# Operand and weight rows of a two-block transformer kernel moved to other SBUF addresses, and its last residual loaded in twelve pieces

## The chip, the cores and the metric

The kernel runs on one NeuronCore of a Trainium2 chip. The metric is the device time of one execution in microseconds (us). PE is the matrix engine (TensorE), DVE the vector engine, ACT the scalar engine, POOL is GpSimd and SP the engine whose queue issues all DMAs here. A partition is one of the 128 lanes of SBUF, the on-chip memory; addresses below are bytes within a partition.

## What is computed

Two transformer blocks over 256 tokens of width 2048 (the first sees 16 more learned tokens ahead of them), all in float32:

```python
# block 1
h = concat([meta, x])                                  # 272 tokens
m = hybrid_mixer(rmsnorm(h, g_pre_mix), w_in, ...)     # two kinds of attention and a convolution; w_out at the end
h = h + rmsnorm(m, g_post_mix)
g = causal_dwconv(rmsnorm(h) @ w_gate, w_conv)         # convolution over three tokens
f = (silu(g) * (rmsnorm(h) @ w_up)) @ w_down           # 2048 -> 5632 -> 2048
h = (h + rmsnorm(f, g_post_ffn))[:, 16:]               # 256 tokens
# block 2
p = rmsnorm(h) @ w_in_2                                # latent attention, top-k attention, gates
h = h + (sigmoid(g1) * (a @ w_branch_a) + sigmoid(g2) * (b @ w_branch_b)) @ w_out_2
q = rmsnorm(h) @ peer_w_q                              # product keys: 16384 experts, top 16 for each of 8 heads
h = h + sum over chosen experts of coef * v_emb        # done densely: U (16384 x 2048), then V
out = rmsnorm(h) * g_final
```

## The kernel before

It is written directly, engine by engine, with semaphores. Nearly all of its time is a stream of weights: the list `PLAN` cuts every weight matrix into chunks of 128 partitions x 1024 columns (8 weight blocks of 128x128, also called rows k here), 1116 in all. Each chunk goes through the same steps, in the order of `PLAN`:

1. SP loads it into `raw` (4 buffers, `RN`), when DVE is done with the chunk four before it (`load`, L725).
2. ACT rounds it to the matmul type float32r into `wh` (3 buffers, `SN`; `cut`, L2091), when PE is done with the chunk three before it.
3. DVE takes the remainder, `wl = raw - wh` (`cut`, L1332).
4. PE multiplies. The operand is split the same way into a high and a low half (`xh`, `xl`), so every 128x128 block takes three matmuls (function `three`):

```python
t.matmul(o, lh, rh, ...)     # L772: weights wh, moving operand xh
t.matmul(o, lh, rl, ...)     # L773: weights wh, moving operand xl
t.matmul(o, ll, rh, ...)     # L774: weights wl, moving operand xh
```

Each has a weight load of its own, which runs while the matmul before it does. ACT and DVE do all else (norms, softmax, convolutions) between their chunks, at slots that tables lay down ahead of time. The order of the work on each engine is fixed when the program is built.

The stages, in this order, with the operand that moves, its columns, and the span of time in the profiled execution:

- first input projection (`in1`), `x`, 272 columns, to 347 us; attention and convolution are mixed into it;
- output projection (`out1`), `y`, 258 columns, 350 to 446 us;
- gate and up (`guk`: the first seven tiles side by side, one k after another; `gu`: the others, tile by tile), `x`, 258 columns for gate tiles and 256 for up tiles, 453 to 958 us;
- down (`down`), `a`, 256 columns, 964 to 1203 us;
- second input projection (`in2k`: seven tiles side by side; `in2`), `x`, 256 columns, 1211 to 1640 us, with the second attention mixed into it; then the branches and the second output projection, to 1815 us;
- `wq` and U, `x`, 256 columns, from 1815 us; from 2410 us U and V alternate; from 2734 us V alone, in which the weights `wh`, `wl` are the moving operand of 512 columns and the coefficients `ch`, `cl` (128x128) are what is loaded.

A gate tile needs `TQ` = 258 columns rather than 256 because the convolution looks two tokens back (`Q0` = 14).

Where buffers start, in the built program (bytes in a partition): `wh` 23200, `wl` 35488, `xh` 47776, `xl` 65440, `yh` 113248, `yl` 129760, `ah` 113248 + 176, `al` 158560 + 176. A chunk is 4096 bytes, so modulo 256 every weight row of 512 bytes starts at 160. `xh` has rows of 276 words (1104 bytes) from its start for the first block, rows of 1024 bytes from word 48 for the second input projection, and from word 28 for `wq` and U (function `normed_at`). `y` has rows of 258 words. "Difference" below is the start of the operand's row less the start of the row of its own weights, modulo 256.

The state of the residual after the second attention is written to HBM (`spill`) and comes back into the `G` tensor as `fin`, with the last gain as `gain`, by two DMAs that SP issues in the middle of the last V half (L757, L758).

Of the kernel before, what the change touches and what calls it, by code (L numbers as in the profile page):

```python
# [17 lines left out]
KT = 16  # L18
# [3 lines left out]
Q0 = 14  # L22
TQ = T1 - Q0
FT = 44
# [44 lines left out]

RN, SN = 4, 3  # L70
CH = 1024

# [100 lines left out]
V1 = AT["V", 0, 1]  # L173
UEND = [AT["U", j, 1] - U0 for j in range(128)]
# [265 lines left out]
def build(nc, A, out):  # L440
# [31 lines left out]
    yh = alloc(mixed_scope, "yh", [128, 16, TQ], F32R)  # L472
    yl = alloc(mixed_scope, "yl", [128, 16, TQ], F32R)
# [24 lines left out]
    ah, al = [alloc(ffn, f"a{i}", [128, 64 + FT * S], F32R)[:, 44:44 + FT * S].rearrange("p (k t) -> p k t", t=S) for i in "hl"]  # L498
# [16 lines left out]
    cosr = alloc(at, "cosr", [128, 2, S])  # L515
    sinr = alloc(at, "sinr", [128, 2, S])
# [32 lines left out]
    oh = alloc(hot_scope, "oh", [128, 8, 2, 128])  # L549
    hot_scope.close()  # L550
    ch, cl = [alloc(px, f"c{i}", [128, 64 + 2 * S], F32R)[:, 28:28 + 2 * S].rearrange("p (n t) -> p n t", t=S) for i in "hl"]
# [30 lines left out]
    hots = [(oh[:, i, 0, :], oh[:, i, 1, :]) for i in range(8)]  # L582
# [137 lines left out]
    def _(y):  # L720
# [19 lines left out]
        for i in range(RN, NCH):  # L740
# [29 lines left out]
    def _(t):  # L770
# [9 lines left out]
        def chunk(i, o, k0, n, rhs, start, stop, ready=None):  # L780

            taken(i)
            for k in range(k0, k0 + n):
                if ready:
                    ready(k)
                c = slice(128 * (k - k0), 128 * (k - k0) + 128)
                last = three(o, wh[:, i % SN, c], wl[:, i % SN, c], *rhs(k), start and k == k0, stop and k == k0 + n - 1)
            last.then_inc(gemm, 1)
# [5 lines left out]
        def pair(i0, outs, rhs, norm):  # L794

            for part in PAIR:
                for i, k in part:
# [5 lines left out]
                    c = slice(128 * (k % 8), 128 * (k % 8) + 128)  # L803
# [1844 lines left out]
```

## Time and profile before

| | |
|---|---|
| median of 3 runs | 3346.98 us (3345.13 to 3348.75) |
| the profiled execution, its own time | 3345.66 us |
| its span, first to last instruction | 3343.8 us |
| PE busy | 3309.1 us, 24828 matmuls |
| DVE busy | 2173.6 us |
| ACT busy | 1678.6 us |
| mean granted clock of PE | 0.995 |
| HBM read | 585.00 MB |

Matmuls overlap in the records: one lasts 0.28 us, but the next starts 0.11 us after it. How fast PE goes is read from how far apart matmuls start, not from their duration, and "busy" says only that some matmul was under way.

### The profile page before, as it was taken

What the parts mean: (1) busy time and instruction counts of PE and PEld (TensorE: products, weight loads), DVE (VectorE), ACT (ScalarE), POOL (GpSimd) and SP (SyncE); (2) the same over time, 40 slices, a digit from 0 to 9 for tenths busy, and PEclk for the clock granted to TensorE, in tenths of its full rate; (3) what the DMA queues carried; (4) which work ended last, traced back from release to release, by engine and by line L of the source; (5) the groups of instructions that cost most, each with busy time, mean ns of one, the idle gap of its engine ahead of it and who ended that gap; (6) DMA issues with size and microseconds to landing.
All of it is one profiled execution on the core that took longest, in us unless ns stands there. A gap on an engine that the chain in (4) does not pass through costs nothing.

```text
span 3343.8 us, 60220 instructions
## 1 busy us (share of the span) xinstructions
PE 3309.1 (99%) x24828; PEld 3136.3 (94%) x24828; DVE 2173.6 (65%) x3664; ACT 1678.6 (50%) x2630; POOL 99.1 (3%) x131
## 2 busy tenths in 40 slices
PE   8999999999999999999999999999999999999998
PEld 8999999999999999899999999999999998888887
DVE  8875367666665477565576698878755555555655
ACT  5454455444444454545455444566644445544544
POOL 0000100000000000000000000122100000000000
PEclk9999999999999999999999999999999999999999
DMA  6433445555566655445566556544555555556554
GB/s 210 139 121 120 158 160 184 184 185 184 180 187 195 195 171 175 136 137 164 183 192 202 196 193 195 178 150 148 162 193 193 192 193 193 193 194 227 189 189 158
DMA packets 164000, 593.12 MB, mean 177 GB/s; under 512 B 18448, under 2 KB 19088, under 8 KB 163344
## 3 DMA queue, kind: packets, MB, share of 16 engines
q1 hardware_dynamic: 163728, 589.27, 54.1%
q8 instruction: 198, 3.24, 0.4%
q14 instruction: 74, 0.61, 0.1%
HBM read 585.00 MB, written 4.19 MB: 176 GB/s over the span
## 4 chain that ended last, share of the span: by engine, by line
PE 98%; DMA 1%; DVE 1%; ACT 0%; SPq 0%; issue 0%; ACTq 0%
PE ps L772 31%; PE ps L773 31%; PE ps L774 30%; PE ps L1260 2%; PE ps L840 1%; PE ps L1061 0%; DMA raw<-in_peer_v 0%; PE ps L1033 0%; PE ps L882 0%; DMA ht<-in_hT 0%; PE ps L810 0%; PE ps L1088 0%; PE ps L842 0%; PE ps L1087 0%; PE ps L1098 0%; PE ps L1083 0%
## 5 line engine op out<-in xcount | busy, mean ns | idle before, releaser
L2091 ACT CAST wh<-raw 128x1024 fp32r<-128x1024 f32 (+2 forms) x1116 | 1163.1, 1043 | 1268.7 <-PE ps L774 1264.6
L1332 DVE TENSOR_TENSOR wl<-raw,wh 128x1024 fp32r<-128x1024 f32 (+2 forms) x1116 | 1347.6, 1209 | 509.4 <-ACT wh L2091 506.9
L772 PE MATMUL ps<-xh,wh 128*128 128x256 f32 (+2 forms) x5184 | 1473.9, 284 | 19.9 <-DVE xl L1341 10.2
L773 PE MATMUL ps<-xl,wh 128*128 128x256 f32 (+2 forms) x5184 | 1454.8, 281 | 0.0
L774 PE MATMUL ps<-xh,wl 128*128 128x256 f32 (+2 forms) x5184 | 1454.3, 281 | 0.0
L772 PEld LDWEIGHTS ps<-xh,wh 128*128 128x128 f32 x5184 | 983.1, 190 | 26.0 <-issue 10.7
L773 PEld LDWEIGHTS ps<-xl,wh 128*128 128x128 f32 x5184 | 983.6, 190 | 2.2
L774 PEld LDWEIGHTS ps<-xh,wl 128*128 128x128 f32 x5184 | 981.1, 189 | 0.0
L772 PE MATMUL ps<-wh,ch 128*128 128x512 f32 x1024 | 400.6, 391 | 1.4 <-DVE cl L2028 1.4
L773 PE MATMUL ps<-wl,ch 128*128 128x512 f32 x1024 | 401.7, 392 | 0.0
L774 PE MATMUL ps<-wh,cl 128*128 128x512 f32 x1024 | 400.8, 391 | 0.0
L2028 DVE TENSOR_TENSOR cl<-G,ch 128x256 fp32r<-128x256 f32 x256 | 109.0, 426 | 245.4 <-ACT ch L2463 245.4
L772 PEld LDWEIGHTS ps<-wh,ch 128*128 128x128 f32 x1024 | 193.8, 189 | 43.4 <-DVE wl L1332 1.8
L774 PEld LDWEIGHTS ps<-wh,cl 128*128 128x128 f32 x1024 | 191.9, 187 | 42.5
L773 PEld LDWEIGHTS ps<-wl,ch 128*128 128x128 f32 x1024 | 192.3, 188 | 39.2
L772 PE MATMUL ps<-ah,wh 128*128 128x256 f32 x704 | 193.6, 275 | 0.0
L773 PE MATMUL ps<-al,wh 128*128 128x256 f32 x704 | 193.6, 275 | 0.0
L774 PE MATMUL ps<-ah,wl 128*128 128x256 f32 x704 | 193.6, 275 | 0.0
L2463 ACT CAST ch<-G 128x256 fp32r<-128x256 f32 x256 | 103.2, 403 | 167.6 <-PE ps L774 167.6
L773 PEld LDWEIGHTS ps<-al,wh 128*128 128x128 f32 x704 | 132.1, 188 | 0.0
L774 PEld LDWEIGHTS ps<-ah,wl 128*128 128x128 f32 x704 | 132.1, 188 | 0.0
L772 PEld LDWEIGHTS ps<-ah,wh 128*128 128x128 f32 x704 | 132.1, 188 | 0.0
(361 smaller groups left out, 3169.6 us busy)
## 6 DMA issues: line engine op xcount, KB each, us to landing
raw<-in_peer_u SPq DMA_DIRECT2D x256, 512.0 KB, 4.3
raw<-in_peer_v SPq DMA_DIRECT2D x256, 512.0 KB, 4.4
raw<-in_w_in SPq DMA_DIRECT2D x186, 512.0 KB, 3.7
raw<-in_w_up SPq DMA_DIRECT2D x82, 512.0 KB, 4.2
raw<-in_w_gate SPq DMA_DIRECT2D x80, 512.0 KB, 4.1
raw<-in_w_down SPq DMA_DIRECT2D x80, 512.0 KB, 4.0
raw<-in_w_out SPq DMA_DIRECT2D x64, 512.0 KB, 3.8
raw<-in_w_branch_a SPq DMA_DIRECT2D x16, 512.0 KB, 3.5
```

The costliest lines, as they stand in the source:

```text
L772: t.matmul(o, lh, rh, start=start, stop=False)
L773: t.matmul(o, lh, rl, start=False, stop=False)
L774: return t.matmul(o, ll, rh, start=False, stop=stop)
L840: t.matmul(dst, qT[rows, c:c + nq], kT[rows, 0:nk], start=True, stop=False)
L1260: t.matmul(ps[5 + n % 3][:, 128 * i:128 * i + 128], b, a, start=True, stop=True).then_inc(hot_mm, 1)
L1332: v.tensor_tensor(wl[:, i % SN, 0:cols(i)], raw[:, i % RN, 0:cols(i)], wh[:, i % SN, 0:cols(i)].bitcast(F32), ALU.subtract).then_inc(lo, 1)
L2028: v.tensor_tensor(cl[:, n % 2, :], G[:, n % 128, :], ch[:, n % 2, :].bitcast(F32), ALU.subtract).then_inc(c_l, 1)
L2091: s.copy(wh[:, i % SN, 0:cols(i)], raw[:, i % RN, 0:cols(i)]).then_inc(hi, 1)
L2463: s.copy(ch[:, n % 2, :], G[:, j, :]).then_inc(c_h, 1)
```

## The change

1. **Wide stages.** For `in1`, `out1` and `gu` each of the 8 weight rows of a chunk starts 144 words (576 bytes) after the one before; the `wh` and `wl` buffers grow from 1024 to 1152 words, and ACT and DVE write them with gaps. The operand of these stages has rows of 272 words (1088 bytes) and starts 28 words (`x`) or 44 words (`y`) into its buffer. The halo grows from 2 to 4 columns (`Q0` = 12), so output projection and gate tiles have 260 columns; up tiles start 4 words into their row, and so do their weights. In `guk` the weights of k start 16 words x (k mod 4) later.
2. **Second input operand.** `x` for the second input projection starts at word 28, not 48. `ah` and `al` become one tensor.
3. **Last residual.** The two DMAs of 128x4096 and 128x2048 words become eight and four of 128x512, one every second chunk, beginning earlier.
4. To pay for the space, cos and sin tables share `gate`, and the one-hot buffers of the expert stage use gaps of `wh`, `wl` and `x` (13 pairs rather than 11).

```diff
-Q0 = 14
+Q0 = 12
+HALO = TQ - S
+PAD_X, PAD_Y, PAD_A, PAD_C = 28, 44, 44, 28
+WIDE = ("in1", "out1", "gu")
+WROW = 144
+PIECE = {AT["V", 10 + 2 * n, 1]: n for n in range(12)}
...
-    wh = alloc(top, "wh", [128, SN, CH], F32R)
-    wl = alloc(top, "wl", [128, SN, CH], F32R)
-    xbuf = [alloc(top, f"x{i}", [128, KT, T1 + 4], F32R) for i in "hl"]
+    wh = alloc(top, "wh", [128, SN, 8 * WROW], F32R)
+    wl = alloc(top, "wl", [128, SN, 8 * WROW], F32R)
+    xbuf = [alloc(top, f"x{i}", [128, KT * (T1 + 4)], F32R) for i in "hl"]
...
-    yh = alloc(mixed_scope, "yh", [128, 16, TQ], F32R)
-    yl = alloc(mixed_scope, "yl", [128, 16, TQ], F32R)
+    yh, yl = [alloc(mixed_scope, f"y{i}", [128, 64 + 16 * T1], F32R)[:, PAD_Y:PAD_Y + 16 * T1].rearrange(
+        "p (k t) -> p k t", t=T1)[:, :, 0:TQ] for i in "hl"]
...
     def normed_at(half, norm):
-        if norm < 2:
-            return xbuf[half][:]
-        o = (48, 28)[norm - 2]
-        return xbuf[half][:].rearrange("p k t -> p (k t)")[:, o:o + KT * S].rearrange("p (k t) -> p k t", t=S)
+        t = T1 if norm < 2 else S
+        return xbuf[half][:, PAD_X:PAD_X + KT * t].rearrange("p (k t) -> p k t", t=t)
+
+    def row_at(w, i, r):
+        name, m, _ = PLAN[i]
+        o = WROW * r + (HALO if name == "gu" and m % 2 else 0) if name in WIDE else 128 * r
+        return w[:, i % SN, o:o + 128]
+
+    def part_at(w, i):
+        name, m, _ = PLAN[i]
+        if name in WIDE:
+            o = HALO if name == "gu" and m % 2 else 0
+            return w[:, i % SN, :].rearrange("p (r c) -> p r c", c=WROW)[:, :, o:o + 128]
+        o = key_row(i)
+        return w[:, i % SN, o:o + cols(i)]
+
+    def key_row(i):
+        name, k, _ = PLAN[i]
+        return 16 * (k % 4) if name == "guk" else 0
...
-            if i == AT["V", 28, 1] + 7:
-                y.wait_ge(d_spill, 16)
-                y.wait_ge(c_l, 128 + 30)
-                y.dma_start(fin, spill).then_inc(d_re, 16)
-                y.dma_start(gain, A["g_final"]).then_inc(d_gf, 16)
+            if i in PIECE:
+                n = PIECE[i]
+                if n == 0:
+                    y.wait_ge(d_spill, 16)
+                y.wait_ge(c_l, 128 + 2 * n + 2)
+                c = slice(512 * (n % 4), 512 * (n % 4) + 512)
+                if n < 8:
+                    y.dma_start(fin[:, n // 4, c], spill[:, n // 4, c]).then_inc(d_re, 16)
+                else:
+                    y.dma_start(gain[:, c], A["g_final"][:, c]).then_inc(d_gf, 16)
...
-        xg = [halves(1, TQ), halves(1, S, 2)]
+        xg = [halves(1, TQ), halves(1, S, HALO)]
...
-            v.tensor_tensor(wl[:, i % SN, 0:cols(i)], raw[:, i % RN, 0:cols(i)], wh[:, i % SN, 0:cols(i)].bitcast(F32),
-                            ALU.subtract).then_inc(lo, 1)
+            v.tensor_tensor(part_at(wl, i), raw_at(i), part_at(wh, i).bitcast(F32), ALU.subtract).then_inc(lo, 1)
...
-            s.copy(wh[:, i % SN, 0:cols(i)], raw[:, i % RN, 0:cols(i)]).then_inc(hi, 1)
+            s.copy(part_at(wh, i), raw_at(i)).then_inc(hi, 1)
```

In the changed program the buffers start at `wh` 23200, `wl` 37024, `xh` 50848 + 112, `xl` 68512 + 112, `yh` 116320 + 176, `yl` 133984 + 176, `a` 116320 + 176. Modulo 256 the first weight row is at 160 and each of these operands at 16, so every difference is 112; only the branches and the second output projection keep 192, and V its own.

The order of the instructions stays as it was on PE, DVE and ACT. It moves on SP, where the last V half is loaded (`raw` is the chunk buffer, `G` holds `fin` and `gain`). SP's queue before, from the last chunk that alternates with U on:

```order
L725 DMA raw<-in_peer_u 128x1024 [waits s_lo] x2
L725 DMA raw<-in_peer_v 128x1024 [waits s_lo] x124
L757 DMA G<-spill 128x4096 [waits s_c_l,s_d_spill]
L758 DMA G<-in_g_final 128x2048
L725 DMA raw<-in_peer_v 128x1024 [waits s_lo] x93
L762 DMA out<-G 128x1024 [waits s_f_out]
```

And the same place of SP's queue in the change; between the fourth row from above and the last but two, the pair of rows goes on in the same way to twelve pieces:

```order
L759 DMA raw<-in_peer_v 128x1024 [waits s_lo] x99
L795 DMA G<-spill 128x512 [waits s_c_l,s_d_spill]
L759 DMA raw<-in_peer_v 128x1024 [waits s_lo] x2
L795 DMA G<-spill 128x512 [waits s_c_l]
...
L797 DMA G<-in_g_final 128x512 [waits s_c_l]
L759 DMA raw<-in_peer_v 128x1024 [waits s_lo] x96
L801 DMA out<-G 128x1024 [waits s_f_out]
```

The 128x4096 and 128x2048 loads stood together behind 124 V chunks; the first small piece now stands behind 99, and two chunks lie between any two pieces.

## Rows read from the trace of the kernel before

**Rows 1.** The page, part 4: the chain that ended last, by engine and line.

```profile
PE 98%; DMA 1%; DVE 1%; ACT 0%; SPq 0%; issue 0%; ACTq 0%
PE ps L772 31%; PE ps L773 31%; PE ps L774 30%; PE ps L1260 2%; PE ps L840 1%; PE ps L1061 0%; DMA raw<-in_peer_v 0%; PE ps L1033 0%; PE ps L882 0%; DMA ht<-in_hT 0%; PE ps L810 0%; PE ps L1088 0%; PE ps L842 0%; PE ps L1087 0%; PE ps L1098 0%; PE ps L1083 0%
```

**Rows 2.** Groups of PE by form: count, busy us, mean ns, idle before.

```profile
L772 PE MATMUL ps<-xh,wh 128*128 128x272 f32 x688 | 205.8, 299 | 9.8 <-DVE wl L1332 9.5 <-DVE xl L1341 0.2
L772 PE MATMUL ps<-xh,wh 128*128 128x258 f32 x704 | 200.0, 284 | 5.0 <-DVE xl L1341 5.0
L772 PE MATMUL ps<-yh,wh 128*128 128x258 f32 x256 | 72.7, 284 | 0.0
```

**Rows 3.** Windows, PE alone: stretch, us, busy (count), clock, DMA share, GB/s.

```profile
34.00:94.00 60.00, 60.00 (x481) 1.00 0.53 174
405.00:440.00 35.00, 35.00 (x294) 1.00 0.55 182
520.00:920.00 400.00, 400.00 (x3330) 1.00 0.56 184
980.00:1180.00 200.00, 200.00 (x1768) 1.00 0.65 193
1880.00:2000.00 120.00, 120.00 (x1061) 1.00 0.57 187
```

**Rows 4.** The same windows view, second input projection.

```profile
1225.00:1245.00 20.00, 20.00 (x172) 1.00 0.57 174
1606.00:1636.00 30.00, 30.00 (x267) 1.00 0.60 186
```

**Rows 5.** Groups of L773 in 1225:1245, 1211:1640 and 1830:2400 us.

```profile
L773 PE MATMUL ps<-xl,wh 128*128 128x256 f32 x57 | 16.0, 281 | 0.0
L773 PE MATMUL ps<-xl,wh 128*128 128x256 f32 x911 | 254.3, 279 | 0.0
L773 PE MATMUL ps<-xl,wh 128*128 128x256 f32 x1471 | 405.4, 276 | 0.0
```

**Rows 6.** Timeline of PE from 1844 us, wq stage: start, us, what.

```profile
1844.33 0.60 PE L1226 MATMUL ps<-ident,ht 128*128 128x128 f32 x4
...
1845.12 0.28 PE L772 MATMUL ps<-xh,wh 128*128 128x256 f32 x1
...
1846.43 0.28 PE L774 MATMUL ps<-xh,wl 128*128 128x256 f32 x1
1846.54 0.28 PE L772 MATMUL ps<-xh,wh 128*128 128x256 f32 x1
```

**Rows 7.** Windows, PE alone, V by itself.

```profile
2760.00:3040.00 280.00, 280.00 (x1237) 1.00 0.59 194
3060.00:3070.00 10.00, 10.00 (x46) 1.00 0.99 406
...
3090.00:3320.00 230.00, 230.00 (x988) 1.00 0.58 188
```

**Rows 8.** The chain in order of time, around 3060 us: start, us, what.

```profile
3057.50 12.21 DMA raw<-in_peer_v
...
3072.53 0.47 PE ps L772
```

**Rows 9.** Timeline of ACT and of PE at the same place.

```profile
3069.74 1.05 ACT L2091 CAST wh<-raw 128x1024 fp32r<-128x1024 f32 x1 [3.59 <-DMA raw<-in_peer_v]
...
3070.75 0.39 PE L774 MATMUL ps<-wh,cl 128*128 128x512 f32 x1
```

**Rows 10.** DMA issues: name, count, KB each, us to landing.

```profile
G<-spill SPq DMA_DIRECT2D x1, 2048.0 KB, 10.7
...
G<-in_g_final SPq DMA_DIRECT2D x1, 1024.0 KB, 12.8
```

**Rows 11.** Windows, all engines (PE, PEld, DVE, ACT, POOL), 60 to 100 us.

```profile
60.00:100.00 40.00, 40.00 (x322) 40.00 (x321) 39.68 (x77) 18.57 (x21) 0.00 (x0) 1.00 0.52 170
```

**Rows 12.** Groups of DVE by form, whole span.

```profile
L1332 DVE TENSOR_TENSOR wl<-raw,wh 128x1024 fp32r<-128x1024 f32 x1062 | 1296.2, 1222 | 475.1 <-ACT wh L2091 472.8
```

More of the change, by code:

```diff
@@ L497, in build @@
     ffn = ExitStack()
-    ah, al = [alloc(ffn, f"a{i}", [128, 64 + FT * S], F32R)[:, 44:44 + FT * S].rearrange("p (k t) -> p k t", t=S) for i in "hl"]
+    ahl = alloc(ffn, "a", [128, PAD_A + 2 * FT * S], F32R)
+    ah, al = [ahl[:, PAD_A + i * FT * S:PAD_A + (i + 1) * FT * S].rearrange("p (k t) -> p k t", t=S) for i in range(2)]
     g_t = alloc(ffn, "g_t", [128, 2, TQ])
@@ L514, in build @@
     perm = alloc(at, "perm", [128, 7, 128])
-    cosr = alloc(at, "cosr", [128, 2, S])
-    sinr = alloc(at, "sinr", [128, 2, S])
+    cosr, sinr = gate[:, 0:2, :], gate[:, 2:4, :]
     rcol = alloc(at, "rcol", [128, 4])
@@ L581, in build @@
     gsum = carve(8)
-    hots = [(oh[:, i, 0, :], oh[:, i, 1, :]) for i in range(8)]
+    spare = [w[:, i, CH:CH + 128] for w in (wh, wl) for i in range(SN)]
+    spare += [x[:, PAD_X + KT * S + 128 * i:PAD_X + KT * S + 128 * i + 128] for x in xbuf for i in range(2)]
+    hots = [(a, oh[:, i, :]) for i, a in enumerate(spare)]
     hots += [(par[:, 256 * i:256 * i + 128], par[:, 256 * i + 128:256 * i + 256]) for i in range(NPAR // 256)]
@@ L785, in chunk @@
                     ready(k)
-                c = slice(128 * (k - k0), 128 * (k - k0) + 128)
-                last = three(o, wh[:, i % SN, c], wl[:, i % SN, c], *rhs(k), start and k == k0, stop and k == k0 + n - 1)
+                last = three(o, row_at(wh, i, k - k0), row_at(wl, i, k - k0), *rhs(k), start and k == k0, stop and k == k0 + n - 1)
             last.then_inc(gemm, 1)
@@ L802, in pair @@
                         t.wait_ge(xlo, 16 * norm + k + 1)
[L803 to L804 removed]
+                    last = three(outs[i], row_at(wh, n, k % 8), row_at(wl, n, k % 8), *rhs[i](k), k == 0, k == 15)
                     if k % 8 == 7:
@@ L1259, in hot_mm_3 @@
                 t.wait_ge(two, tk + 1)
-                t.matmul(ps[5 + n % 3][:, 128 * i:128 * i + 128], b, a, start=True, stop=True).then_inc(hot_mm, 1)
+                t.matmul(ps[5 + n % 3][:, 128 * i:128 * i + 128], b, a.bitcast(F32), start=True, stop=True).then_inc(hot_mm, 1)
         def side_3(name, a):
@@ L1611, in side_g @@
                 v.wait_ge(gu_t, f + 1)
-                v.scalar_tensor_tensor(c1, g1[:, 1:1 + S], w[1], c1, ALU.mult, ALU.add).then_inc(own.up(), 1)
+                v.scalar_tensor_tensor(c1, g1[:, HALO - 1:HALO - 1 + S], w[1], c1, ALU.mult, ALU.add).then_inc(own.up(), 1)
                 v.wait_ge(own.sem, own.n)
-                v.scalar_tensor_tensor(c1, g1[:, 2:2 + S], w[2], c1, ALU.mult, ALU.add).then_inc(gu_c, 1)
+                v.scalar_tensor_tensor(c1, g1[:, HALO:HALO + S], w[2], c1, ALU.mult, ALU.add).then_inc(gu_c, 1)
             elif name == "u":
@@ L2265, in side_g @@
                     s.wait_ge(gu_m, f - 1)
-                s.activation(c1, g_t[:, f % 2, 0:S], ACT.Copy, scale=pc("w_ffn_conv", 3 * f)).then_inc(gu_t, 1)
+                s.activation(c1, g_t[:, f % 2, HALO - 2:HALO - 2 + S], ACT.Copy, scale=pc("w_ffn_conv", 3 * f)).then_inc(gu_t, 1)
             elif name == "conv":
```

16 lines of the change are left out of this document (9 added, 7 removed).

## The prediction

> **What bounds the kernel now.** I read the page's chain first: 98% of the span is PE, and nearly all of that is the three lines of `three` [rows 1]. DVE and ACT are about two thirds and half busy, so a microsecond is gained only if the matmuls follow each other faster or an idle hole in PE closes. Holes are few: PE is busy in every stretch of the windows that I read [rows 3, 4]. So the question is how far apart matmuls start. The windows view gives that: length of the stretch over its count, after taking off the 2.4 matmuls (1.7 for 512 columns) that began before the stretch, because one lasts 0.28 us (0.39) and is counted where it overlaps.
>
> - Down projection (256 columns): 200 us / 1765.6 = 113.3 ns. The U stage gives the same (120/1058.6 = 113.4) [rows 3].
> - First projection (272 columns): 60/478.6 = 125.4 ns. Output projection (258): 35/291.6 = 120.0. Gate and up tiles (258 and 256 alternately): 400/3327.6 = 120.2 [rows 3].
> - V halves (512 columns): 280/1235.3 = 226.7 ns early, 230/986.3 = 233.2 late [rows 7]. 226.7 is twice 113.3, so the fast pace is proportional to columns, 0.443 ns each. By it 272 columns would take 120.4, 260 take 115.1, 258 take 114.2.
>
> The three wide stages thus lose 5 to 7 ns per matmul against a pace that other stages hold, at full granted clock in all of them. What is different there? From the sizes of the buffers in their order of allocation I worked out where the moving operand's row starts relative to the weights' row, modulo 256 bytes. Down projection: 112. Second input projection: 192. wq and U: 112. All have operand rows of 1024 bytes beside weight rows of 512, so the difference is the same for every k. In the wide stages operand rows are 1104 (x) or 1032 (y) bytes, and the difference wanders by 80 or 8 per k.
>
> The pace isn't a matter of the difference alone. The second input projection has a constant 192 and does both: 20/169.6 = 117.9 ns in its first part and 30/264.6 = 113.4 at its end [rows 4]. The duration of one shows it too: 281 ns at the slower pace; over the whole stage the xl matmuls average 279.1 (254.3 us / 911), where wq and U, side work included, have 275.6 (405.4/1471) [rows 5]. At 112 an interruption costs only a short run: after four identity matmuls the starts are 119 ns apart for 11 steps (1845.12 to 1846.43), and the next comes after 0.11 us [rows 6], as all do from there. I read this as two streams, moving operand and next weights, that lock into a free relation if the addresses repeat, and that from 112 always find it.
>
> Against it stands the Trainium skill ("TensorE: Matmul & The Clock Gate", Step-by-step: what each phase is for): the weight load has its own read port and doesn't steal bandwidth from the running matmul. By that, addresses could not matter. The rows differ: the same instruction with the same shape takes 113.3 or 117.9 ns. What it would make of the time is the first rival below.
>
> **The change, part by part.**
> 1. *Wide stages.* Rows of 1088 bytes beside rows of 576: both step by 64 modulo 256, so a matmul and its own weights differ by 112 for every k, and so for y, and for up tiles, where operand and weights both start 16 bytes later. If they lock: first projection 2064 matmuls (three times 688 [rows 2]) x (125.4 - 120.4) = 10.3 us; output projection 768 x (120.0 - 115.1) = 3.8; gate 2112 x (120.2 - 115.1) = 10.8; up 2112 x (120.2 - 113.3) = 14.6. Sum 39.5 us. The two extra columns are already in it: 2880 matmuls x 2 x 0.443 = 2.6 us.
>    Off it: each interruption costs some 14 matmuls x 5 ns = 0.07 us [rows 6]; the attention in the first projection makes about 50 (estimate: five groups for each of ten heads), 3.3 us; changes between gate and up tiles, 2 us (I take half of what 81 changes at 0.05 would cost). DVE has 39.68 of 40 us busy between 60 and 100 us [rows 11]: when a chunk falls from 3.01 to 2.89 us, DVE can't follow there, 1 us. That leaves 33 us.
> 2. *Strided conversions.* wh and wl are written as 8 rows of 128 with gaps. No row shows such a write. A 128x1024 subtraction takes 1222 ns contiguous [rows 12]. Lower bound nothing; upper bound a tenth more for the 86 in the first projection, 86 x 0.122 = 10.5 us, because only there DVE has no cover. In gate and up a chunk has 24 x 115 = 2760 ns, which covers both engines. I take nothing, as the data per lane are the same number of contiguous words in each row.
> 3. *Second input operand* from 192 to 112. 2736 matmuls (three times 912, of which [rows 5] has 911); the stage's mean duration would fall from 279.1 to 275.6, and between 275.6 and 281 lie 4.5 ns of spacing: 2.9 ns x 2736 = 8 us at most, nothing at least (if 112 re-locks no better in a stage that is interrupted every 24 to 48 matmuls). I take 3.5.
> 4. *Twelve pieces.* The 2048 KB and 1024 KB loads stand ahead of a raw load, which then lands after 12.21 us; ACT waits 3.59 us for it and PE's next matmul after 3070.75 starts at 3072.53, 1.78 us where 0.23 is normal: 1.55 us [rows 8 to 10]. And the pace changes at just that place: 226.7 before it, 233.2 after [rows 7]. The rest, 3072.5 to 3332 us, is 1113 matmuls x 6.5 = 7.2 us. A piece is 256 KB per two chunks of 512 KB: 194 GB/s becomes about 243, and the crowded stretch shows 406 GB/s [rows 7], so no stall should follow. One-hot buffers, the shared cos/sin and the joined a tensor add nothing: no engine on the chain waits for them. Sum 8.8 us.
>
> The profiled execution has 3345.66 us (span 3343.8), 1.3 under the median. 3345.7 - 33 - 3.5 - 8.8 = 3300.4; with half of the 1.3, **3301 us**.
>
> **The rivals.**
> - *No address effect.* The paces come from the operand's length or the stage. Then the extra columns cost 2.6 us, the pieces give 1.55 or 8.8: 3337 to 3345 us. For it: no row shows 258 or 272 columns with a constant difference, so none shows them fast over a stretch. Against it: the second input projection and V at two paces. Chance 0.10. The Trainium skill's rule (same page and section as above) would end here.
> - *Only 256-column tiles lock.* 272 and 260 columns don't fit the rhythm that 256 and 512 share; up tiles gain (14.6 less 2), gate, input and output projections only pay 2.6: 3345.7 - 12.6 + 2.6 - 3.5 - 8.8 = 3323. Against it nothing but that no row tests it. Chance 0.13.
> - *One in three is off.* The third matmul of each k runs while the next k's weights load, 576 bytes on: its difference is 48, where at 1024/512 it stays 112. At the slow pace for a third: 39.5 x 2/3 - 4 = 22 us instead of 33: 3311. Chance 0.15.
> - *DVE becomes the bound in the first projection* (part 2's upper bound): 3301 to 3311, inside the others; 0.05.
> - *Slower: V locks badly from its start.* At 2734 us V stands alone at 226.7; nothing in the rows says why it fell there. Had it entered at 233.2, the stretch to 3071 would cost 1487 x 6.5 = 9.7 us, and the 7.2 would not come back. Wide stages locked: 3345.7 - 33 - 3.5 - 1.55 + 9.7 = 3317 (0.07). Wide stages not locked: 3345.7 + 2.6 - 1.55 + 9.7 = 3356 (0.04). It decides the sign when the wide stages bring under 10.7 us.
>
> **How the numbers follow.** The sum as worked out, 3290 to 3306, has 0.46; 3311 has 0.20 with the DVE case; 3317 and 3323 have 0.20; 3337 to 3345 has 0.10; 3356 has 0.04. The range 3290 to 3328 holds 0.84. The low end is the full 39.5 + 8 + 8.8 = 56.3 (3290). 0.2% is 6.7 us, about what a measurement of this kernel can tell. Faster (under 3340): 0.92 and a little less for what I don't see, 0.91; same 0.05; slower 0.04.
>
> **What would show it.** Right: windows give about 120.4 to 121.5 ns in the first projection, 115 in the output projection, 114 to 115 in gate/up, 113.3 to 115 in the second input projection, 226.7 through V to the end, and no long landing near 3000 us. "One in three" shows as 122 and 117; "only 256" as 125, 121 and about 118 in gate/up; no effect as 125, 121, 121. A DVE bound shows as PE idle behind wl. V at 233 from 2700 us on would make 3301 wrong by 17 us.

## The result and the profile after

The changed kernel takes 3343.99 us (median of 12 runs, 3335.44 to 3347.21) where the kernel before takes 3349.9 on the same chip (12 runs, 3341.5 to 3356.02). The medians lie 5.9 us apart; the ratio of the two sets of runs is 0.9977, 95% interval 0.9966 to 0.9988: faster by 4 to 11 us. I had forecast 49 us (3301 against the 3350 measured here, 46 against the 3347 that I started from), and 0.91 for a time under 3340. The direction is right, the size is not, and the time lies outside the range of 3290 to 3328.

The page of the changed kernel, part 4, the chain that ended last (`three` is now L811 to L813):

```profile
PE ps L811 31%; PE ps L812 30%; PE ps L813 30%; PE ps L1297 2%; PE ps L877 1%; PE ps L1098 0%; DVE wl L1369 0%; PE ps L1070 0%; PE ps L919 0%; PE ps L847 0%; PE ps L1125 0%; PE ps L879 0%; PE ps L1124 0%; PE ps L881 0%; PE ps L1135 0%; PE ps L1120 0%
```

The raw load of `peer_v` that stood in the chain of before [rows 1] is gone from it. The rest is the same stream of matmuls. Windows, PE alone (stretch, us, busy and count, granted clock, DMA share, GB/s), over the stretches that [rows 3], [rows 4] and [rows 7] show of before:

```profile
34.00:94.00 60.00, 60.00 (x481) 1.00 0.52 173
405.00:440.00 35.00, 35.00 (x293) 1.00 0.55 183
520.00:920.00 400.00, 400.00 (x3349) 1.00 0.56 185
1225.00:1245.00 20.00, 20.00 (x179) 1.00 0.61 187
2760.00:3040.00 280.00, 280.00 (x1237) 1.00 0.60 202
3060.00:3070.00 10.00, 10.00 (x46) 1.00 0.60 197
3090.00:3320.00 230.00, 230.00 (x1016) 1.00 0.59 191
```

Read as in the prediction (length over the count less 2.4, less 1.7 in V):

| stage | before, ns per matmul | forecast | after |
|---|---|---|---|
| first projection | 125.4 | 120.4 to 121.5 | 125.4 |
| output projection | 120.0 | 115 | 120.4 |
| gate and up | 120.2 | 114 to 115 | 119.5 |
| second input projection, 1225 to 1245 us | 117.9 | 113.3 to 115 | 113.3 |
| V before 3071 us | 226.7 | 226.7 | 226.7 |
| V after it | 233.2 | 226.7 | 226.8 |

So in these windows the last two parts of the change did what was said of them (experiments 3 and 10 take some of that back), and the first, from which 33 of the 45 us were to come, did nearly nothing. The strided conversions cost nothing, as taken: groups of DVE and of ACT by form.

```profile
L1369 DVE TENSOR_TENSOR wl<-raw,wh 128x1024 fp32r<-128x1024 f32 x1062 | 1297.1, 1223 | 476.9 <-ACT wh L2127 474.6
L2127 ACT CAST wh<-raw 128x1024 fp32r<-128x1024 f32 x1062 | 1116.9, 1052 | 1198.8 <-PE ps L813 1198.6
```

1223 ns against 1222 [rows 12]. The DMA issues of the residual and the gain are twelve, and land in 5 us each:

```profile
G<-spill SPq DMA_DIRECT2D x8, 256.0 KB, 4.9
G<-in_g_final SPq DMA_DIRECT2D x4, 256.0 KB, 5.3
```

**Where the two traces differ, stage by stage**, by the start of the last matmul of each: V 599.2 to 590.2 us (9.0 less: the hole and the pace); second input projection up to the second output projection 611.3 to 610.2 (1.1 less); gate and up with the norm ahead of it 517.5 to 515.5 (2.0 less); down, `wq` and U unchanged. Against that the first two stages end 8.6 us later (454.7 for 446.1 us), and but for some 0.3 us of the wider output projection this isn't the work of the change: three kernels below that have the code of before up to here (vzero2, pieces and narrow) end them at 447, 452 and 454 us. Windows of the attention part, the first of the kernel before, the second of the changed one:

```profile
110.00:340.00 230.00, 230.00 (x1644) 0.97 0.38 124
```

```profile
110.00:340.00 230.00, 230.00 (x1588) 0.93 0.36 118
```

The mean granted clock is 0.97 and 0.93 of 2.4 GHz: in a part of this stretch, where small matmuls of attention stand between the large ones, the clock was at 1.2 GHz, and for longer in this execution than in that. 56 matmuls fewer at some 0.14 us are 8 us. How long these dips are changes from execution to execution of any of the kernels below (the same window counts 1586 to 1644 matmuls in their profiles, a spread of 8 us; 1634 in the second profile of the changed kernel, experiment 10, whose output projection ends at 448.3 us), and it is why one profiled execution can't be set against another as a whole. The medians can.

### The profile page after: what moved, and what is told of

The parts are those of the page before. It is cut to its first block, busy times and chain, and to the rows that moved or that the text cites. A ratio compares the mean times of both kernels' runs of the same rounds, so it can differ in the third digit from the quotient of the medians.

```text
span 3340.5 us, 60230 instructions
## 1 busy us (share of the span) xinstructions
PE 3306.8 (99%) x24828; PEld 3137.8 (94%) x24828; DVE 2174.9 (65%) x3664; ACT 1677.8 (50%) x2630; POOL 100.8 (3%) x131
## 4 chain that ended last, share of the span: by engine, by line
PE 98%; DVE 1%; ACT 0%; DMA 0%; issue 0%; SPq 0%; ACTq 0%
PE ps L811 31%; PE ps L812 30%; PE ps L813 30%; PE ps L1297 2%; PE ps L877 1%; PE ps L1098 0%; DVE wl L1369 0%; PE ps L1070 0%; PE ps L919 0%; PE ps L847 0%; PE ps L1125 0%; PE ps L879 0%; PE ps L1124 0%; PE ps L881 0%; PE ps L1135 0%; PE ps L1120 0%
## 5 line engine op out<-in xcount | busy, mean ns | idle before, releaser
L1369 DVE TENSOR_TENSOR wl<-raw,wh 128x1024 fp32r<-128x1024 f32 (+2 forms) x1116 | 1348.5, 1210 | 511.1 <-ACT wh L2127 508.1
L811 PE MATMUL ps<-xh,wh 128*128 128x256 f32 (+2 forms) x5184 | 1474.8, 284 | 20.0 <-DVE xl L1377 10.2
L813 PE MATMUL ps<-xh,wl 128*128 128x256 f32 (+2 forms) x5184 | 1453.4, 280 | 0.0
L811 PEld LDWEIGHTS ps<-xh,wh 128*128 128x128 f32 x5184 | 982.7, 190 | 26.3 <-issue 11.0
L813 PEld LDWEIGHTS ps<-xh,wl 128*128 128x128 f32 x5184 | 980.2, 189 | 0.0
L811 PE MATMUL ps<-wh,ch 128*128 128x512 f32 x1024 | 398.7, 389 | 0.0
L813 PE MATMUL ps<-wh,cl 128*128 128x512 f32 x1024 | 398.5, 389 | 0.0
L813 PEld LDWEIGHTS ps<-wh,cl 128*128 128x128 f32 x1024 | 192.2, 188 | 40.4
L811 PEld LDWEIGHTS ps<-wh,ch 128*128 128x128 f32 x1024 | 192.2, 188 | 38.9 <-issue 0.7
L812 PE MATMUL ps<-a,wh 128*128 128x256 f32 x704 | 193.6, 275 | 0.0
L811 PE MATMUL ps<-a,wh 128*128 128x256 f32 x704 | 193.6, 275 | 0.0
L813 PE MATMUL ps<-a,wl 128*128 128x256 f32 x704 | 193.6, 275 | 0.0
L811 PEld LDWEIGHTS ps<-a,wh 128*128 128x128 f32 x704 | 132.2, 188 | 0.0
L812 PEld LDWEIGHTS ps<-a,wh 128*128 128x128 f32 x704 | 132.2, 188 | 0.0
L813 PEld LDWEIGHTS ps<-a,wl 128*128 128x128 f32 x704 | 132.2, 188 | 0.0
```

The source lines that it names most:

```text
L811: t.matmul(o, lh, rh, start=start, stop=False)
L812: t.matmul(o, lh, rl, start=False, stop=False)
L813: return t.matmul(o, ll, rh, start=False, stop=stop)
L1369: v.tensor_tensor(part_at(wl, i), raw_at(i), part_at(wh, i).bitcast(F32), ALU.subtract).then_inc(lo, 1)
```

## The experiments

Experiments 1, 4, 5 and 11 are benchmarks: they run the matmuls alone and ask which addresses, row lengths and neighbours give which pace. The others are whole kernels: 2, 3 and 6 take the change apart, 7 to 9 use starts that the benchmarks point to, and 10 repeats the changed kernel. Code is cut to the lines that matter; a row length such as 256/128 is that of the operand and of the weights, in words of 4 bytes.

### 1. The matmuls alone (bench1)

This and the other benchmarks compute nothing of the reference. The program has 66 series; the 70 of the expectation was a miscount.

```diff
+for n, (cols, xs, ws, diff, both) in enumerate(cases()):     # 66 series of 96 matmuls
+    for tile in range(2):
+        for k in range(16):
+            a, b = wh[:, w0:w0 + 128], wl[:, w0:w0 + 128]    # w0 steps by ws words per k
+            h, l = xh[:, x0:x0 + cols], xl[:, x0:x0 + cols]  # x0 steps by xs words, starts diff bytes on
+            t.matmul(o, a, h, ...); t.matmul(o, a, l, ...); t.matmul(o, b, h, ...)
+    # two matmuls on a matrix of ones
```

> This kernel computes nothing of the reference: it loads one block of w_gate, fills wh, wl, xh and xl with it, and runs 70 short series of 96 matmuls with the same triple (wh/xh, wh/xl, wl/xh), each series with other columns, row steps and difference of addresses; two identity-free 128x128 matmuls stand between series. The changed kernel's wide stages ran at 125.0, 120.5 and 119.5 ns per matmul, not at 120.4, 115.1 and 114. Theory A (the step): what locks is a step of both rows by a multiple of 256 bytes, so that the next weights, too, keep their difference; then 272 columns lock at about 120.4 ns if the operand rows are 1280 bytes and the weight rows 512, and 256 columns don't lock with rows of 1088 and 576 (about 118). Theory B (the length): only 256 or 512 columns fit the rhythm; then 258, 260 and 272 columns run 5 to 6 ns over 0.443 ns a column (120, 121 and 126 ns) with any rows, 1024/512 and 1280/512 too, and 256 columns lock with rows of 1088 and 576. Theory C (no address effect at all): every series of 256 columns runs at one pace. The sweep of the difference at 1024/512 shows which differences lock: 112 surely (113.3), 192 perhaps at 117.8.

Measured, as the mean distance of starts in the second half of a series (ns; rows in words, operand/weights):

| columns | rows | difference | ns |
|---|---|---|---|
| 256 | 256/128 | 112 | 113.3 |
| 256 | 256/128 | fifteen others, 0 to 240 in steps of 16 | 116.7 to 120.0 |
| 256 | 256/128 | 116, 120 | 121.8, 122.2 |
| 256 | 272/128 | 112 | 118.6 |
| 256 | 256/144 | 112 | 116.6 |
| 272, 260, 256 | 272/144 (the change) | 112 | 124.9, 120.5, 118.3 |
| 272, 258, 256 | 276/128 (before) | 0, 0, 8 | 125.1, 119.7, 120.6 |
| 258, 272, 512 | 256/128 | 112 | 120.1, 126.7, 231.1 |
| 256 | 320/128 | 112 | 113.3 |
| 272 | 320/128 | 112, 160, 192, six others | 123.4, 123.3, 123.3, 125.4 to 126.7 |

Windows of the series 256/128 at 112, and of 272/128 at 112 (the second by its length of rows):

```profile
431.00:437.00 6.00, 6.00 (x55) 1.00 0.01 3
```

```profile
297.00:307.00 10.00, 10.00 (x87) 1.00 0.00 0
```

6/52.6 = 114 ns and 10/84.6 = 118 ns (a count of such a short window is good to 2 ns; the table has the starts themselves). What follows: with nothing else running, addresses alone move the same matmul from 113.3 to 122 ns, so there is an address effect. But the changed kernel's three shapes have here just the paces that it has in its trace. 272 words modulo 64 is 16, as is 144, so the difference stays 112 for every k, and that isn't enough: whatever must repeat, it is not the difference alone. The 113.3 appeared only with 256 columns and both rows a multiple of 256 bytes.

### 2. The twelve pieces alone (pieces)

```diff
-            if i == AT["V", 28, 1] + 7:
-                y.dma_start(fin, spill).then_inc(d_re, 16)
-                y.dma_start(gain, A["g_final"]).then_inc(d_gf, 16)
+            if i in PIECE:
+                ... one of 12 pieces of 512 columns, every second V chunk
```

> The kernel before with the twelve pieces alone. My theory: no landing over 6 us in the V half, no hole of 1.8 us, and V at 226.7 ns per matmul to its end instead of 233.2 from 3071 us on: 8.8 us less, ratio 0.9974. Rival 1 (the load was hidden but for the hole): 1.5 us less, ratio 0.9995, V at 233 somewhere. Rival 2 (more packets slow the raw loads): no gain or a loss.

Median 3349.66 (11 runs) beside 3349.85 (21 runs) of before, ratio 0.9992, interval 0.9983 to 1.0001. The hole is gone, the 8.8 us are not there; of the three theories the first rival (0.9995, V at 233 somewhere) fits. Windows of V:

```profile
2760.00:3040.00 280.00, 280.00 (x1237) 1.00 0.60 202
3090.00:3110.00 20.00, 20.00 (x90) 1.00 0.56 193
...
3150.00:3310.00 160.00, 160.00 (x688) 1.00 0.56 188
```

20/88.3 = 226.5 ns and then 160/686.3 = 233.1: V goes past 3072 us at the fast pace and loses it some 60 us later. The timeline shows where (PEld is the weight load of the matmul after it):

```profile
3123.30 0.41 PE L778 MATMUL ps<-wh,ch 128*128 128x512 f32 x1
3123.55 0.39 PE L779 MATMUL ps<-wl,ch 128*128 128x512 f32 x1
3123.78 0.39 PE L780 MATMUL ps<-wh,cl 128*128 128x512 f32 x1
...
3132.98 0.69 DVE L2066 TENSOR_TENSOR G<-G 128x512 f32<-128x512 f32 x1 [0.79 <-ACT G L2485]
3133.59 0.42 DVE L2034 TENSOR_TENSOR cl<-G,ch 128x256 fp32r<-128x256 f32 x1
3134.12 0.19 PEld L778 LDWEIGHTS ps<-wh,ch 128*128 128x128 f32 x1 [0.16 <-issue]
3134.22 0.40 PE L778 MATMUL ps<-wh,ch 128*128 128x512 f32 x1
3134.46 0.40 PE L779 MATMUL ps<-wl,ch 128*128 128x512 f32 x1
```

At 3123.5 us one start comes 250 ns after the last instead of 227, and within two matmuls the pace is 226.7 again. At 3134.5 us one comes only 239 ns after the last, and the stream is in the slow pace from then on. A delay of 12 ns is enough to cost 6.5 ns on each of the 860 or so matmuls that are left, and one of 23 ns isn't always.

Where the delays come from can be read beside them: DVE adds up the residual (`G<-G`, 0.69 us, four times, 5.5 us apart), the low half `cl` of the coefficients comes behind it and ends at 3134.01 us, and PE's weight load, idle for 0.16 us, starts at 3134.12. In all seven profiles that have such a late start, it comes 0.45 us after the end of a `cl` subtraction behind one of these additions. That PE waits for `cl` there is inferred from these times; the trace names no wait.

### 3. The pieces and the second input operand (narrow)

```diff
-        o = (48, 28)[norm - 2]
+        o = 28
```

> The kernel before with the twelve pieces and the second input operand at word 28, without the wide rows and the larger halo. If the wide rows bring nothing (as the changed kernel's paces say), this is as fast as the changed kernel or a few us faster: pieces 8.8 us and second operand 2 to 4 us, 3338 against a before of 3350, ratio 0.9965. If the wide rows do bring something that the clock's dips hid in the one profile, this is slower than the changed kernel by that, ratio 0.998 or more.

Median 3347.41 (11 runs), ratio 0.999, interval 0.9981 to 0.9999, not the 0.9965 of the first theory. V falls to 233 ns here too, after a start that comes 245 ns after the last at 3124.3 us. The stage from 1210 to 1821 us takes 610.9 us where it takes 611.5 with the pieces alone: 0.6 us for the operand, and 1.1 by before and after. The fast window of the table above (117.9 to 113.3) is a short stretch; over the stage the gain is a third of what I took.

### 4. Tiles in turn, and 512 columns (bench2)

```diff
+pairs: ("320/128 up at 112", gate (260 columns, 96), up (256, 112)), ("320/128 up at 192", (260, 176), (256, 192)),
+       ("272/144", ...), ("276/128", ...)                   # 12 tiles of 48, nothing between them
+wide:  512 columns, operand and weights as in V; between two series, two matmuls of 8 to 192 columns
```

> A microbenchmark: it leaves the whole computation of the reference out and writes sums of its own; only the pace of its matmuls is read. First four times twelve tiles of 48 matmuls, gate-like (260 or 258 columns) and up-like (256 columns) in turn and without anything between them, with rows of 320/128, 320/128, 272/144 and 276/128 words (operand/weights); then 48 series of 512 columns, weights as the moving operand as in V, with two matmuls on a matrix of ones between them. Theory A (256 columns lock when both rows step by multiples of 256 bytes and the difference is 112): the up tiles of the first group reach 113.3 ns in the middle of each tile, mean 115 to 116 over the tile with the run-in; the second group (difference 192) 118 to 119, the third 118 to 119.5, the fourth 119 to 120. Theory B (lock is lost for good by what the gate tile leaves): all four groups 118 to 120. For 512 columns: if V's pace is bistable, series at difference 240 give 226.7 in some and 233 in others, depending on the length of what stands between (8 to 192 columns); if the difference decides, all 24 series at 240 give one value and the sweep over 16 differences shows which ones are fast.

Windows inside the four groups:

```profile
72.00:100.00 28.00, 28.00 (x236) 1.00 0.01 1
140.00:170.00 30.00, 30.00 (x258) 1.00 0.00 1
205.00:240.00 35.00, 35.00 (x295) 1.00 0.00 1
275.00:310.00 35.00, 35.00 (x293) 1.00 0.00 1
```

119.9, 117.4, 119.6 and 120.4 ns, gate and up together. Both theories miss. The up tiles at 112, which had 113.3 in the first benchmark when they came after the ones, have 120.0 throughout when they come after a gate tile at 96. The up tiles at 192, a difference that had 117.8 alone (rows 256/128), run at 113.3 from the sixth matmul on after a gate tile at 176 (113.9 over the tile). So one and the same shape at one and the same address has more than one pace, and what ran before picks it. The 512-column series say the same: at 240, V's difference, 20 of 24 interruptions lead to 236.8 ns, and those of 136, 152, 168 and 184 columns to 233.3; none leads to the 226.7 that V has in the kernel until 3072 us. At 112, the series behind one at 240 and 192 columns runs at 226.7; the seven behind another at 112 and 16 to 112 columns run at 231.

### 5. All starts (bench3)

```diff
+pairs():   258 or 260 columns at d - 8 or d - 16, then 256 at d; d = 0, 16, ... 240; rows 320/128
+singles(): 272 and 258 columns, 16 differences, two interruptions
+wide():    512 columns, 32 differences, two interruptions
```

> A microbenchmark that leaves the whole computation of the reference out; only the pace of its matmuls is read. 32 groups of gate-like and up-like tiles in turn (258 or 260 columns, then 256, rows of 320 words beside 128, the up tile's difference from 0 to 240 bytes in steps of 16); 64 single tiles of 272 or 258 columns after two different interruptions; 64 series of 512 columns at differences from 0 to 248 in steps of 8 after two different interruptions. Theory A (the relation of the two streams has several states that hold themselves up, and which one is entered depends on what ran before): the fast up tile of the second benchmark (113.3 ns at 192 after a 260-column tile at 176) repeats, other differences give up tiles at 113.3 too, but not all; single tiles and 512-column series change their pace with the interruption at one and the same difference, 226.7, 231 and 233 to 237 ns for 512. Theory B (the address difference alone decides): the same difference gives the same pace for both interruptions and for both widths of the tile before.

Windows of two groups of 258 and 256 columns, the up tiles at 112 and at 192:

```profile
290.00:314.00 24.00, 24.00 (x204) 1.00 0.00 1
462.00:487.00 25.00, 25.00 (x219) 1.00 0.00 1
```

119.0 and 115.4 ns. By the starts the whole groups have 119.5 and 116.3, the first tile of each, slow from the interruption before it, included; without that tile 119.0 and 115.2 (gate 117.8, up 113.3 in the latter). Of 32 groups only three have up tiles under 114 (192 with either width, 64 with 258 columns). Single tiles of 272 columns: 123.2 and 123.4 at 112, 124.3 at 208, 124.7 to 126.8 elsewhere, 160 and 192 included, which had 123.3 in the first benchmark; of 258 columns: 116.7 to 116.8 at 16 and 64, 117.4 at 96, up to 122.2 at 240. 512 columns: 226.7 at 0 and 228.8 at 64, after both interruptions; the other thirty lie between 230 and 237, and at four of the 32 (104, 152, 168, 232) the two interruptions give paces that differ by 0.9 to 3.4 ns. Both theories have a part of it: most differences give one pace whatever stood before, some don't.

### 6. The change without the pieces (whole)

```diff
-            if i in PIECE:
-                ... the twelve pieces
+            if i == AT["V", 28, 1] + 7:
+                ... the two loads of before
```

> The changed kernel with one part undone: the residual and the gain are loaded as 2048 KB and 1024 KB again, where the twelve pieces were. Theory A (the gain of the change over the version without the wide rows is mostly V's pace, which the pieces alone don't secure): the hole of 1.5 us is back, V falls to 233 ns at about 3072 us and stays there, and the median is 8 to 9 us over the changed kernel's, that is level with the kernel before or 1 us above it (3348 to 3352 on the chip of the first runs). Theory B (the wide rows bring 3.4 us, as the difference between the changed kernel and the one without them suggests, and the pieces 0 to 1): 3344 to 3346, 4 to 5 us under before. A V that stays at 226.7 in spite of the hole would speak for the addresses of the weights (their slots now lie 4608 bytes apart) as what holds V's pace.

Median 3348.04 (11 runs) beside 3350.7 (15 runs), ratio 0.9991, interval 0.9982 to 1.0. The hole (1.56 us from one start to the next at 3077 us, 1.78 before) and the 233 ns after it are back:

```profile
3090.00:3110.00 20.00, 20.00 (x88) 1.00 0.61 185
...
3150.00:3310.00 160.00, 160.00 (x688) 1.00 0.60 188
```

The first theory expected the time about level with before, and 0.9991 fits it as well as the 3 us that gate and up (2.0) and the second operand (1.1) give by the traces. The other half of the expectation missed: the changed kernel's ratio is 0.9977, so the pieces are worth some 5 us in it (0.0014), not 8 to 9 and not 0 to 1; experiment 10 shows why it lies between.

### 7 and 8. Rows and starts from the benchmark, and the same rows with bad starts (lock, offbeat)

```diff
+XROW, XBUF, CPOS, YPOS = 320, 5184, 4160, 20     # offbeat: 4164, 4
-    xbuf = [alloc(top, f"x{i}", [128, KT, T1 + 4], F32R) for i in "hl"]
+    xbuf = [alloc(top, f"x{i}", [128, XBUF], F32R) for i in "hl"]
+    y: rows of XROW words from word YPOS;  ch, cl = x[:, CPOS:CPOS + 2 * S]
+        o, t = ((28, XROW), (46, XROW), (28, S), (28, S))[norm]      # offbeat: (32, ...), (26, ...)
```

> The kernel before, with operand rows of 1280 bytes in the first projection, the output projection and gate/up (weights stay at 512, so both steps are multiples of 256 bytes), and start differences taken from the third benchmark: 112 in the first projection (272 columns, 123.3 ns there against 125), 16 in the output projection (258 columns, 116.8 against 120), 184 for gate tiles and 192 for up tiles (117.8 and 113.3, mean of a pair 116.3, counted with the changes between tiles; before's pace is 120.2), 0 for V (226.7); second operand at 112 and the twelve pieces too. For room, some scratch tensors share memory and there are 15 pairs of one-hot buffers for 19. Theory A (several states that hold themselves up; rows that repeat modulo 256 and the right start enter the good one): gate/up 4224 x 3.9 = 16.5 us, output projection 768 x 3.2 = 2.5, first projection 2064 x 1.7 = 3.5 at most, V 226.7 from 2734 us to its end, 7 to 8, the hole 1.5: 28 to 32 us under the kernel before, a ratio of 0.991 to 0.992. Theory B (benchmarks have a quiet chip; in the kernel, with DMA and four engines writing, such states don't hold): gate/up 119 to 120, V back to 233 after some event near 3123 us, 0.997 to 0.999.

> The same kernel with only the starts of the operands moved by a few words, to differences that the benchmarks show as slow: 128 in the first projection (126.7 ns), 208 in the output projection (120.0), 104 and 112 in gate/up (mean of a pair 119.4), 240 in V (233 to 237). Nothing else differs, row lengths and sizes are the same. Theory A: slower than the other one by 4224 x 3.1 = 13 us in gate/up, 7 in the first projection, 2.5 in the output projection and up to 9 in V, 25 to 32 us in all, so level with the kernel before (ratio 0.998 to 1.002). Theory B (the start doesn't matter in the kernel): both the same within 3 us. A V at 226.7 in spite of 240, entered from the stage before it, is possible, and then the difference is 18 to 23 us.

The first takes 3324.52 us (6 runs) beside 3350.5 (17 runs): ratio 0.9922, interval 0.9907 to 0.9937. The second takes 3343.01 (11 runs): 0.998, interval 0.9971 to 0.9989. Windows, first of lock, then of offbeat:

```profile
34.00:94.00 60.00, 60.00 (x486) 1.00 0.54 175
405.00:435.00 30.00, 30.00 (x260) 1.00 0.58 188
520.00:920.00 400.00, 400.00 (x3423) 1.00 0.60 190
...
3150.00:3310.00 160.00, 160.00 (x708) 1.00 0.56 183
```

```profile
34.00:94.00 60.00, 60.00 (x476) 1.00 0.54 173
405.00:435.00 30.00, 30.00 (x249) 1.00 0.56 181
520.00:920.00 400.00, 400.00 (x3379) 1.00 0.59 187
...
3150.00:3310.00 160.00, 160.00 (x687) 1.00 0.60 189
```

| stage | lock: benchmark, kernel | offbeat: benchmark, kernel |
|---|---|---|
| first projection | 123.3, 124.1 | 126.7, 126.7 |
| output projection | 116.8, 116.5 | 120.0, 121.7 |
| gate and up | 116.3, 116.9 | 119.4, 118.5 |
| V after 3150 us | 226.7, 226.5 | 233 to 237, 233.5 |

The two programs do the same work in the same order with buffers of the same size; only starts differ, by 16 to 80 bytes, and the medians by 18.5 us. That is the address effect, shown in the kernel. The benchmark's paces carry over within 2 ns (the 116.3 and 119.4 have the slow first tile in them; without it 115.2 and 119.0). In V, lock comes back to 226.7 after each of the four additions of the residual (a start 247 ns after the last at 3107 us, ten disturbed ones from 3118 us on); offbeat, at 240, comes back after the first (255 ns, at 3120 us) and falls after the second, at 3126 us. The sum of the expectation (28 to 32 us) was 2 to 6 too high: gate and up took 504.5 us for 517.5 (13.0 rather than 16.5), since 0.6 ns more per matmul are 2.5 us. What the first projection brought of its 3.5 can't be told from one trace, since the clock dips there cost more than that.

### 9. One number in V (vzero2)

```diff
-    ch, cl = [alloc(px, f"c{i}", [128, 64 + 2 * S], F32R)[:, 28:28 + 2 * S] ...
+    ch, cl = [alloc(px, f"c{i}", [128, 64 + 2 * S], F32R)[:, 24:24 + 2 * S] ...
```

> The kernel before with one number changed: V's stationary operand starts 16 bytes earlier, so that V's difference is 0 where it was 240. The hole at 3071 us stays (the two big loads are untouched). Theory A (at 0 the fast relation of V is found again after any interruption, as in both series of the third benchmark; at 240 it isn't): the same 226.7 ns from the hole to the end, 1113 matmuls x 6.5 ns = 7.2 us under the kernel before, a ratio of 0.9978; in the stretch before 2734 us, where V and U take turns, nothing or 1 us more. Theory B (V falls to 233 because of what runs beside it after 3072 us, not because of the addresses): the trace shows 233 after the hole again, ratio 0.999 to 1.001.

Median 3341.68 (9 runs) beside 3350.82 (18 runs), ratio 0.9978, interval 0.9968 to 0.9988: the forecast of 0.9978, and as much as the whole change under study brings. The hole is still there (1.88 us at 3073 us), and so is a start 244 ns after the last at 3121 us. After both the pace is 226.7:

```profile
3090.00:3320.00 230.00, 230.00 (x1016) 1.00 0.60 190
3150.00:3310.00 160.00, 160.00 (x707) 1.00 0.62 194
```

### 10. The changed kernel once more (again2)

The same program, with a comment at its end.

> The changed kernel once more, to see how much of its time repeats. Theory A (its V is at difference 240, where the fast pace survives or falls at the small events near 3123 and 3134 us by chance of a few ns, as it fell in the two kernels with pieces alone and with pieces and the moved operand): the ratio is 0.9965 to 0.999 again, and the trace may show V at 226.7 to the end or at 233.3 from one of these events on; first projection 125, output projection 120.5, gate/up 119.5, the same as in its first trace. Theory B (the wide weights' slots, 4608 bytes apart, keep V at 226.7): the trace shows 226.7 to the end again, and no kernel with slots 4096 bytes apart and difference 240 does.

Median 3341.34 (10 runs), ratio 0.9977, interval 0.9968 to 0.9987, the first result again. In this trace V comes through a start 256 ns after the last at 3116 us and falls at 3121 us, at the second addition of the residual, though no start there is more than 4 ns late before the fall:

```profile
3090.00:3110.00 20.00, 20.00 (x90) 1.00 0.60 202
3090.00:3320.00 230.00, 230.00 (x992) 1.00 0.57 185
3150.00:3310.00 160.00, 160.00 (x688) 1.00 0.57 188
```

The other paces are those of the first trace (481, 293 and 3350 in its windows). So one program has both ends in V. The first trace has the same disturbances, starts 250 and 242 ns after the last at 3123 and 3134 us, and came back to 226.7 after all four additions; of the kernels at 240 that are at 226.7 when the additions begin, narrow falls at the first of the four, this one and offbeat at the second, pieces at the third. That V stayed at 226.7 in the first trace was luck, and the wide weights' slots don't hold it there.

### 11. The change's rows at every start (bench4)

```diff
+pairs():   260 or 258 columns at d, then 256 at d; d = 0, 16, ... 240; rows 272/144
```

> A microbenchmark that leaves the whole computation of the reference out; only the pace of its matmuls is read. The changed kernel's row lengths, 272 words for the operand beside 144 for the weights: 32 groups of gate-like and up-like tiles in turn (260 or 258 columns, then 256), both at one difference, from 0 to 240 bytes in steps of 16; then 32 single tiles of 272 or 258 columns. The changed kernel has 112 (pair mean 119.5). Theory A (a good relation needs rows that repeat modulo 256 bytes; a start doesn't cure the others): no group has an up tile under 116 ns, and the best pair mean is 118 or more, where rows of 320 beside 128 had 116.3. Theory B (the change's rows were as good as any, only its start of 112 was wrong): some start brings up tiles to 113.3 and a pair mean of 116 to 117 here too.

The best of 32 groups has a mean of 117.9 ns with its slow first tile and 117.5 without it (up 116.9, at 64), the best up tiles settle at 116.1 (at 0 and 176); at 112, the change's start, the mean is 119.9 and 119.4. Windows of the groups at 64 and at 112:

```profile
180.00:208.00 28.00, 28.00 (x241) 1.00 0.00 1
285.00:313.00 28.00, 28.00 (x237) 1.00 0.01 1
```

117.3 and 119.4 ns. The first theory holds but for the best mean, 0.1 to 0.5 ns under its 118: with rows of 1088 beside 576 bytes no start gives what rows of 1280 beside 512 give. A start of 64 rather than 112 might be worth 2 ns, 8 us in gate and up (estimate: 4224 matmuls); that was not run in the kernel.

## Why the prediction was wrong, point by point

- **"If they lock", the wide stages: wrong, and most of the miss (31 of some 38 us).** The step reads: rows of 1088 bytes beside 576 both step by 64 modulo 256, so a matmul and its own weights differ by 112 for every k, and so the stages lock at 0.443 ns a column. The paces are 125.4, 120.4 and 119.5 instead of 120.4, 115 and 114 to 115. The term of 33 us measured 2.0, all of it in gate and up and with the extra columns paid; the other two stages show no gain in pace. Two things in it are wrong. I had seen the free pace only with 256 and 512 columns and with rows that are multiples of 256 bytes, and took the one thing out of three that the change keeps, the difference. The benchmarks show that the others matter: at a difference of 112, 258 columns have 120.1 ns and 272 have 126.7 even with rows of 1024 and 512; and 256 columns have 118.6 or 116.6 when only one of the two rows steps otherwise. And "from 112 always find it" is wrong too: 112 is left at 120.0 behind a gate tile at 96.
- **The rival "only 256-column tiles lock"** had the columns right, for V and the 320/128 rows, and would have given 3323 us; it kept the same wrong condition on the rows, and the up tiles fell short as well (118.4 with rows 272/144).
- **The rival "no address effect"** gave 3337 to 3345 us, and the median lies in it; the rule of the Trainium skill ("TensorE: Matmul & The Clock Gate", Step-by-step: what each phase is for), a read port of its own for the weight load, would end there. That addresses don't matter is refuted: lock and offbeat differ in starts alone, and by 18.5 us. Whether it is the weight load that the moving operand collides with, no run shows. I gave it 0.10, and the time came near for another reason: the effect exists, and the change misses its conditions.
- **"One in three is off" (0.15) and the DVE bound (0.05) didn't happen.** The first was to show as 122 and 117; the paces are 125.4 and 120.4. For the second, PE was idle behind `wl` for 9.4 us in the 272-column matmuls, 9.5 before [rows 2]; since the stage got no faster, the bound wasn't put to the test.
- **Strided conversions: right.** 1223 ns for 1222.
- **Second input operand: 3.5 us taken, about 1 measured** (611.3 to 610.2; 0.6 by experiments 2 and 3). The range of 0 to 8 held it. "If 112 re-locks no better in a stage that is interrupted" was the right doubt.
- **Twelve pieces: 8.8 us taken.** The hole of 1.55 is gone in each kernel with the pieces. The 7.2 of pace come in one trace of the changed kernel (the full 9.0 in V), and not in the other one, nor in pieces and narrow: V falls at 3121, 3134 and 3124 us there. The step "the pace changes at just that place" was a true reading with a wrong cause: the hole is the largest of several delays, down to some ns, that can throw V out of its pace at a difference of 240. Experiment 9 takes the cause away and leaves the hole: the 7.2 us are there.
- **"V locks badly from its start": didn't happen** in any trace; from 2734 us V stands at 226.7 each time.
- **The sum, mended.** 2.0 + 1.1 + 1.55, and in V between 1.4 (some 215 matmuls until a fall at 3121 us, 6.5 ns each) and 7.2: 6 to 12 us, against 7.7 by the ratio. The extra 1.3 us between the profiled execution of before and its median, of which I took half, was no sound correction: the clock dips between 110 and 340 us alone move a single execution by more.

What stays open: why just these addresses and columns give a free relation, and what decides whether V comes back to its pace after a small delay: at 240, starts 250 and 256 ns after the last were survived and one of 239 was not. The benchmarks list the paces; they don't explain them.

## What to carry to other kernels

When one and the same matmul has two paces in a trace, don't infer the condition of the fast one from what the fast stages share; there are always several such things. Run the matmuls alone, in the order in which the kernel has them and with its interruptions, over all starts: benchmarks of 0.7 to 2.1 ms found most of the 18 us by which lock beats the change under study. Prefer a start that has the fast pace after every interruption tried (V at 0) over one that has it after some (V at 240), and compare such kernels by medians, since a trace shows only one of the ways in which it can go.

## What the runs showed of the hardware

- float32r matmuls of 256 columns follow each other at 113.3 to 122.9 ns, and of 512 columns at 226.7 to 236.8, at full granted clock, depending on the start of the moving operand's row relative to the weights' row modulo 256 bytes, on the row steps, and on what ran before.
- The pace can have several values that hold themselves up at one address: 512 columns at 240 run at 236.8 ns after most interruptions, at 233.3 after 136, 152, 168 and 184 columns, and at 226.7 in V until it is disturbed; at 112 they run at 226.7 or 231. A delay of 12 ns in a stream can cost 3% from there on (pieces, 3134 us), and one of 23 ns can cost nothing (the changed kernel, 3123 us).
- 258 columns never ran at the pace per column of 256: at best 115.5 ns over half a tile, where 0.443 ns a column would be 114.2; 272 at best 122.8 for 120.4.
- The granted clock dips in the part with small attention matmuls in every profiled execution, and for times that differ: its mean between 110 and 340 us is 0.93 to 0.97.
